# A decode step on one core: page sums taken in quarters ahead of the weight splits, the sample's output and branch A's heads moved

## The reference

```
proj = einsum('bsd,de->bse', rmsnorm(x), w_in)
q, k, v, g_a, u, v_s, g_b, m_a, m_b = split(proj)
attn   = moba(q, k, v, ...)            # branch A, 8 heads of 64
sgu    = gelu(u) * (tril(w_s) @ layernorm(gelu(v_s)) + b_s)   # branch B
y_a, y_b = attn * silu(g_a), sgu * silu(g_b)
mixed  = sigmoid(m_a) * (y_a @ w_pa) + sigmoid(m_b) * (y_b @ w_pb)
out    = rmsnorm(x + mixed @ w_o)
```

## Time and profile before

| | |
|---|---|
| median of 3 runs | 613.47 us |
| the profiled execution's own time | 611.43 us |
| its span, first to last instruction | 609.5 us |
| mean granted clock of PE | 0.992 |
| PE busy | 575.8 us, 94% of the span, 6242 matmuls |
| DVE busy | 313.1 us, 51%, 690 instructions |
| ACT busy | 215.4 us, 35%, 470 instructions |
| DMA, hardware queue | 55.9% of 16 engines' span |

### The profile page before, as it was taken

How to read it: one execution, slowest core, us unless ns; L and a number is a source line. 1 busy time by engine, 2 the same in 40 slices (tenths; PEclk the granted TensorE clock), 3 DMA queues, 4 the chain that set the end, 5 groups by cost and what they waited for, 6 DMA issues and landing times.

```text
span 609.5 us, 15236 instructions
## 1 busy us (share of the span) xinstructions
PE 575.8 (94%) x6242; PEld 540.3 (89%) x6242; DVE 313.1 (51%) x690; ACT 215.4 (35%) x470; POOL 28.9 (5%) x40
## 2 busy tenths in 40 slices
PE   3799998999999999999999999999999989999993
PEld 2799998999899989989889988998999979999993
DVE  5533131434555744855766574694463263692316
ACT  5422321233434423454354541241153241233243
POOL 1310121100000000000000000011000000000002
PEclk9999998999999999999999999999999999999998
DMA  8437333455766767568576668884779857222103
GB/s 289 129 86 279 106 108 105 126 160 186 221 182 207 225 200 243 181 195 254 174 223 203 188 222 248 274 252 157 239 261 317 257 158 260 88 95 94 46 0 147
DMA packets 73990, 112.50 MB, mean 185 GB/s; under 512 B 5417, under 2 KB 38194, under 8 KB 73922
## 3 DMA queue, kind: packets, MB, share of 16 engines
q1 hardware_dynamic: 72690, 108.18, 55.9%
q0 software_dynamic: 1232, 3.36, 1.8%
HBM read 106.98 MB, written 4.53 MB: 183 GB/s over the span
## 4 chain that ended last, share of the span: by engine, by line
PE 80%; DVE 12%; ACT 4%; issue 2%; DMA 1%; POOL 0%; DVEq 0%; SPq 0%; ACTq 0%; POOLq 0%
PE BK L470 47%; PE BK L590 8%; PE BK L490 7%; PE BK L602 4%; PE BK L616 4%; PE BK L666 2%; DVE WL L1022 1%; PE BK L683 1%; PE BK L673 1%; DMA XR<-in_x_prompt 1%; DVE XR L1043 1%; ACT SC L913 1%; DVE NMX L1210 1%; ACT APX L926 1%; PE BK L642 1%
## 5 line engine op out<-in xcount | busy, mean ns | idle before, releaser
L470 PE MATMUL BK<-XH,WH 128*128 128x272 f32 x704 | 224.3, 319 | 1.6 <-POOL WL L1455 1.6
L470 PE MATMUL BK<-XH,WL 128*128 128x272 f32 x704 | 204.5, 291 | 0.0
L470 PE MATMUL BK<-XL,WH 128*128 128x272 f32 x704 | 203.5, 289 | 0.0
L470 PEld LDWEIGHTS BK<-XH,WH 128*128 128x128 f32 x704 | 133.9, 190 | 12.4 <-issue 9.2
L470 PEld LDWEIGHTS BK<-XL,WH 128*128 128x128 f32 x704 | 134.4, 191 | 0.5 <-issue 0.5
L470 PEld LDWEIGHTS BK<-XH,WL 128*128 128x128 f32 x704 | 133.7, 190 | 0.0
L1022 DVE TENSOR_TENSOR WL<-WRAW,WH 128x1024 fp32r<-128x1024 f32 x58 | 71.0, 1224 | 96.5 <-ACT WH L815 96.3
L590 PE MATMUL BK<-CST,KRAW 128*128 128x128 f32 x512 | 77.1, 273 | 2.4 <-DVE ATS L1196 2.2
L1116 DVE COPY KT<-BK 128x512 f32<-128x512 f32 x64 | 44.2, 691 | 57.0 <-PE BK L590 56.9
L815 ACT ACTIVATE WH<-WRAW 128x1024 fp32r<-128x1024 f32 x60 | 63.2, 1054 | 21.3 <-PE BK L490 21.3
L590 PEld LDWEIGHTS BK<-CST,KRAW 128*128 128x128 f32 x512 | 60.1, 140 | 4.4 <-issue 4.1
(11 more groups left out here) (186 smaller groups left out, 780.3 us busy)
## 6 DMA issues: line engine op xcount, KB each, us to landing
KRAW<-in_cache_k SPq DMA_DIRECT2D x128, 256.0 KB, 3.3
VRAW<-in_cache_v SPq DMA_DIRECT2D x120, 256.0 KB, 3.8
WRAW<-in_w_in SPq DMA_DIRECT2D x22, 1024.0 KB, 5.5
WRAW<-in_w_o SPq DMA_DIRECT2D x4, 1024.0 KB, 5.2
XR<-in_x_prompt SPq DMA_DIRECT2D x4, 512.0 KB, 6.7
VEX<-in_cache_v SPq DMA_DIRECT2D x8, 256.0 KB, 4.0
WRAW<-in_w_pb SPq DMA_DIRECT2D x4, 512.0 KB, 6.8
WRAW<-in_w_pa SPq DMA_DIRECT2D x4, 512.0 KB, 5.9
```

The source lines that it names most:

```text
L470: last = mm(BK[h][:, 0:HALF], w[:, n % 2, k, :], x[:, k, cols], start=(i == 0 and w is WH and x is XA), stop=(i == KC - 1 and w is WL))
```

## The change

DVE's `block_sums` becomes `page_sums`, which after each fourth step's scores reduces those four pages (128 elements a row) to a sum and a maximum; after the fourth quarter it adds the bias of the last page and goes on to `gate_rows`, as before. It stands, with `prompt_out`, in front of `split_lo`. `sample_out` moves from t % 16 = 6 to 5 (the last one, t = 140, stays), ahead of that step's gelu and spatial work. On ACT, `exponentials` goes ahead of `gelu_tanh`. The heads of branch A are split in four pieces at t = 133 to 136 instead of one at t = 130, and PE's waits count the pieces.

```diff
--- before.py
+++ after.py
@@ -736,7 +736,7 @@
                 for u in range(16):
                     n, x, h = unit_of(u)
                     if u < 2:
-                        pe.wait_ge(yal_ok, u + 1)
+                        pe.wait_ge(yal_ok, PAIRS + u)
                     yield from branch(n, x, h, 16 + u, XH, XL)
 
             fill = filling()
@@ -957,10 +957,10 @@
                     page_out(t)
                 if t % 4 == 1 and 53 <= t < 85:
                     gelu_square((t - 53) // 4)
+                if t % 16 == 2 and t > 16 and t < 144:
+                    exponentials(t // 16 - 1)
                 if t % 4 == 2 and 54 <= t < 86:
                     gelu_tanh((t - 54) // 4)
-                if t % 16 == 2 and t > 16 and t < 144:
-                    exponentials(t // 16 - 1)
                 if t % 4 == 3 and 19 <= t < 83:
                     prompt_exp(t // 4 - 4)
                 if t % 4 == 0 and 20 <= t < 84:
@@ -968,10 +968,12 @@
                 if t == 111:
                     act.wait_ge(yb_ok, 5)
                     copy(YBH[:], G[:, GB:GB + 4, :]).then_inc(ybh_ok, 1)
-                if t == 130:
+                if 133 <= t < 133 + PAIRS:
+
+                    c = t - 133
                     act.wait_ge(av_ev, 16)
                     act.wait_ge(pj, matmuls_before(T_PB))
-                    copy(XH[:, 0:4, 0:SEQ], G[:, GA:GA + 4, 0:SEQ]).then_inc(yah_ok, 1)
+                    copy(XH[:, c, 0:SEQ], G[:, GA + c, 0:SEQ]).then_inc(yah_ok, 1)
                 if t == 141:
                     act.wait_ge(ya_ok, 1)
                     copy(XH[:, 0:4, SEQ:ROWS], G[:, GA:GA + 4, SEQ:ROWS]).then_inc(yah_ok, 1)
@@ -1142,13 +1144,24 @@
                 dve.wait_ge(ge_dve, 2 * (4 + c) + 2)
                 dve.tensor_tensor(G[:, GB + c], G[:, GB + c], G[:, GU + c], ALU.mult).then_inc(ug_ok, 1)
 
-            def block_sums(b):
-                dve.wait_ge(sc_pe, 4 * b + 4)
-                sc = SCB[:].rearrange("p (x n) -> p x n", x=4)
-                link(dve.tensor_reduce(KP[:, 0, :], sc, AX.X, ALU.add))
-                last_page = SCB[96:128, 3 * P:4 * P]
-                link(dve.tensor_tensor(last_page, last_page, B15, ALU.add))
-                link(dve.tensor_reduce(KP[:, 1, :], sc, AX.X, ALU.max))
+            def page_sums(q):
+
+                b, x = q // 4, q % 4
+                dve.wait_ge(sc_pe, q + 1)
+                if x == 0:
+                    wait(dve, r_ok, b)
+                sc = SCB[:, x * P:(x + 1) * P]
+                summed = dve.tensor_reduce(KP[:, 0, x:x + 1], sc, AX.X, ALU.add)
+                if x == 3:
+                    link(summed)
+                    last_page = SCB[96:128, 3 * P:4 * P]
+                    link(dve.tensor_tensor(last_page, last_page, B15, ALU.add))
+                peak = dve.tensor_reduce(KP[:, 1, x:x + 1], sc, AX.X, ALU.max)
+                if x == 3:
+                    link(peak)
+                    gate_rows(b)
+
+            def gate_rows(b):
                 own, pair, kp = CST[:, C_OWN:C_OWN + 4], CST[:, C_PAIR:C_PAIR + 2], KP[:]
                 dve.tensor_tensor(R[:, 0:8].rearrange("p (x j) -> p x j", x=4), bass.AP(pair.tensor, pair.offset, [list(pair.ap[0]), [0, 4], [1, 2]]),
                                   bass.AP(kp.tensor, kp.offset, [list(kp.ap[0]), [1, 4], [0, 2]]), ALU.mult)
@@ -1318,6 +1331,11 @@
                 if t % 4 == 0 and 4 <= t <= 128:
                     if T_GA <= n - 1 < T_GMA or T_GB <= n - 1 < T_GMB:
                         silu(n - 1, 1)
+                if t % 4 == 0 and 4 <= t <= PAGES:
+                    page_sums(t // 4 - 1)
+                if t % 4 == 0 and 20 <= t < 84:
+                    prompt_out(t // 4 - 5)
+                if t % 4 == 0 and 4 <= t <= 128:
                     split_lo(n + 1)
                 if t % 4 == 2 and t < 128 and (T_GA <= n < T_GMA or T_GB <= n < T_GMB):
                     silu(n, 0)
@@ -1330,7 +1348,7 @@
                     dve.wait_ge(ot_ev, NB)
                     dve.tensor_tensor(G[:, GA:GA + 4, SEQ:ROWS], G[:, GA:GA + 4, SEQ:ROWS], ATS[:], ALU.mult).then_inc(ya_ok, 1)
                 if t == 142:
-                    dve.wait_ge(yah_ok, 2)
+                    dve.wait_ge(yah_ok, PAIRS + 1)
                     dve.tensor_tensor(XL[:, 0:4, SEQ:ROWS], G[:, GA:GA + 4, SEQ:ROWS], f32(XH[:, 0:4, SEQ:ROWS]), ALU.subtract).then_inc(yal_ok, 1)
                 if t % 16 == 2 and t >= 34:
                     scale_out(t // 16 - 2)
@@ -1340,18 +1358,14 @@
                     page_out(t)
                 if t % 4 == 2 and 22 <= t < 86:
                     prompt_gate(t // 4 - 5)
-                if t % 16 == 6 and t >= 38:
-                    sample_out(t // 16 - 2)
-                if t % 16 == 0 and t >= 16 and t < 144:
-                    block_sums(t // 16 - 1)
                 if t % 16 == 1 and t >= 16 and t < 144:
                     choose(t // 16 - 1)
+                if t % 16 == 5 and t >= 37:
+                    sample_out(t // 16 - 2)
                 if t % 4 == 2 and 18 <= t < 82:
                     prompt_max(t // 4 - 4)
                 if t % 4 == 3 and 19 <= t < 83:
                     prompt_norm(t // 4 - 4)
-                if t % 4 == 0 and 20 <= t < 84:
-                    prompt_out(t // 4 - 5)
                 if t % 4 == 1 and 53 <= t < 85:
                     gelu_inner((t - 53) // 4)
                 if t % 4 == 3 and 55 <= t < 87:
@@ -1371,9 +1385,10 @@
                 if t == 111:
                     dve.wait_ge(ybh_ok, 1)
                     dve.tensor_tensor(YBL[:], G[:, GB:GB + 4, :], f32(YBH[:]), ALU.subtract).then_inc(ybl_ok, 1)
-                if t == 130:
-                    dve.wait_ge(yah_ok, 1)
-                    dve.tensor_tensor(XL[:, 0:4, 0:SEQ], G[:, GA:GA + 4, 0:SEQ], f32(XH[:, 0:4, 0:SEQ]), ALU.subtract).then_inc(yal_ok, 1)
+                if 133 <= t < 133 + PAIRS:
+                    c = t - 133
+                    dve.wait_ge(yah_ok, c + 1)
+                    dve.tensor_tensor(XL[:, c, 0:SEQ], G[:, GA + c, 0:SEQ], f32(XH[:, c, 0:SEQ]), ALU.subtract).then_inc(yal_ok, 1)
                 if t >= 129:
                     mixed_b(t - 129)
             mixed_b(15)
```

## The result

The changed kernel takes 614.28 us (median of 20 runs, 611.93 to 617.38), the kernel before 611.32 (20 runs, 610.0 to 614.92). The ratio on record for the two is **1.0033, 95% interval 1.0018 to 1.0049**: slower by 2.0 us of 611, with 1.1 to 3.0 as the interval. The two medians are 3.0 us apart, at the interval's upper end; I go by the ratio. Its profiled execution took 613.03 us, its span is 611.1 us against 609.5, PE is busy 575.2 us of it (575.8 before).

A forecast was written before the change was run, and what follows sets the result against it. PE is busy 94% of the span, so only its waits move the time. Lost 4.9 us, won 4.7, net +0.2 on the 613.47 median: 613.7 us, range 611.8 to 616.4.

The forecast's parts named there:

- prompt gate, t = 66: PE's 0.9 us wait for the prompt gate stays but shrinks by 0.18 us, counted as -0.2.
- gate sums, t = 17 to 20: PE comes to the choice 0.55 us earlier at t = 17 but waits 0.5 there: 0.05 us won.
- exponentials, t = 81 to 83: ACT's exponentials ahead of gelu's tanh cut PE's lateness from 1.10 to 0.04 us: -1.2 us.
- after page 127: PE's wait for page sums at t = 129 goes, 0.43 us; branch A's heads in pieces win 0.3 us.
- The new wait behind the prompt copy: At t = 20, 36, 52, 68 the split delays LT, making PE's page turning 1.13 us late each: +4.5 us.
- The later choice: DVE's gate copy GS comes 0.2 us later, delaying PE's prompt gate at t = 34 and 50: +0.4 us.
- The quarters' price: Each DVE reduction of 128 elements was taken to cost 0.286 us; quarters by themselves cost nothing where DVE is idle.
- rival (b): DVE falls behind in more places if a quarter's reduction costs 0.68 us, deciding from about 0.32: 616.0 us; chance 0.17.
- the sample's output one step earlier: PE's two waits for ATS go, 1.48 us at t = 85 and another 1.05 late: -2.5 us.
- Rival (a): Earlier sums reach the exponentials, so the waits at t = 99, 115, 131 go, 2.8 us: 610.9 us; chance 0.15.
- Rival (c): The clock falls after each of the four new waits, 1.7 us each, +6.7: 620.4 us; chance 0.08.
- Rival (d): Sums in front free nobody; gains and losses both stay under 1 us: 613.5 us; chance 0.05.

The follow-up runs named there:

- (2): Kernel before with only DVE's prompt copy put ahead of the weight split at t % 16 = 4 (four steps): ratio 1.0057.
- (1): Kernel before with only the quarter sums, placed in front of the weight split: ratio 0.9981.
- (8): Kernel before with only ACT's exponentials ahead of gelu's tanh: ratio 0.9978.
- experiment 4: Kernel before with only the sample's output taken out one step earlier: ratio 0.9978.
- 5: Changed kernel with SP's loads of mixing weights, gating constants and layernorm rows at t = 83 instead of 84: ratio 1.0009 against the kernel before.
- 7: Kernel before with the sample's output one step earlier and SP's loads of mixing weights and constants at t = 83: ratio 0.9944.
- experiment 9: Kernel before with only branch A's heads split in four pieces at t = 133 to 136: ratio 0.9994.
- experiment 10: Kernel of 6 with, at t = 97, 113, 129, gate sums ahead of page turning and choice ahead of page copy: ratio 0.9909 against the kernel before.
- 3: Changed kernel with the weight split back ahead of the prompt copy at t % 16 = 4: ratio 0.9952 against the kernel before.
- 6: Changed kernel with the split back ahead of the prompt copy at t % 16 = 4 and the loads at t = 83: ratio 0.9930 against the kernel before.

## Why the prediction was right, and where not

The prediction was 613.7 us and no change that can be told, with a range that holds the 614.28 measured. It gave most to "same" (0.53), and more to slower (0.29) than to faster (0.18). The lean was right, but its number was too kind: +0.2 us worked out, +1.47 in the trace from the first page, and a ratio whose interval, 0.18% to 0.49%, lies almost wholly past the 0.2% I had set as the limit of "same".

```
step                          worked out   trace     single experiment
pages 21, 37, 53, 69 (LT)       +4.5       +4.57     +4.5 (2)
prompt gate, t = 34, 50         +0.4       +0.44
prompt gate, t = 66             -0.2       -0.23
gate sums, t = 17 to 20          0.0        0.0      0.0 (1)
exponentials, t = 81 to 83      -1.2       -1.38     -1.14 (8)
output, t = 86, 102             -2.5       -2.58     -2.53 (4)
mixing weights, t = 87            -        +1.42     gone with the load moved (5, 7)
after page 127                  -0.7       -0.71     -0.20 of it the pieces (9)
```

The trace's column is the page table above, cut at the steps; the numbers in brackets are the experiments.

- **The new wait behind the prompt copy** was right in place, number and size. LT's end and the release 0.15 us behind it came as worked out.
- **The later choice** was right too. GS follows the prompt turning by APT, WL and KT, each overlapped by 0.09, as the changed kernel's DVE rows show beside the earlier trace rows:

```profile
201.59 0.69 DVE L1238 COPY APT<-BK 128x512 f32<-128x512 f32 x1 [0.83 <-PE BK L673]
202.20 1.22 DVE L1024 TENSOR_TENSOR WL<-WRAW,WH 128x1024 fp32r<-128x1024 f32 x1
203.33 0.68 DVE L1118 COPY KT<-BK 128x512 f32<-128x512 f32 x1
203.93 0.17 DVE L1173 COPY GS<-BK 128x24 f32<-128x24 f32 x1
```

- **The quarters' price**: 0.286 was taken for a reduction; the changed kernel has

```profile
L1154 DVE TENSOR_REDUCE KP<-BK 128x1 f32<-128x128 f32 x32 | 9.3, 291 | 46.3 <-PE BK L602 46.3
...
L1159 DVE TENSOR_REDUCE KP<-BK 128x1 f32<-128x128 f32 x32 | 9.1, 283 | 0.3
```

so rival (b), which needed over 0.32, falls, and the thin margins at t = 84 and 116 held.
- **The step that failed** is "the sample's output one step earlier: the 1.48 us go ... -2.5 us in all". The waits went, but what is late next was not looked for. It was a load on SP's queue, issued at t = 84 behind four value pages, that in the trace of before had landed 0.2 us ahead of its reader at t = 87. With 1.42 us for it the sum would have been +1.6 us, 615.1 against the median I started from.
- **At t = 17 to 20** the sum was right, one part of it was not named: of the gain at the gate sums, 0.55 worked out and 0.57 in the trace, some 0.25 us is lost at once at page 18, which waits for GS, and the other 0.3 at t = 19.
- Rival (a) falls: the waits at t = 99, 115 and 131 stayed, 0.37, 0.81 and 1.70 us late as before, until experiment 10 moved the gate sums themselves.
- Rival (c) falls: the granted clock is 1.00 after each of the four new waits (in the stretches 164 to 168, 216 to 220, 268 to 272 and 320 to 324 us). Rival (d) falls with the sizes above.

That the level of the runs moved, from 613.47 in three runs to 611.32 in twenty, has nothing to do with the change; the last section shows two causes of such differences, though not which of them made those three runs high. By the new level the forecast of +0.2 would read 611.5 and the +1.47 of the trace 612.8. So it is partly luck that 613.7 lies so near the measured 614.28: the level carried over was 2 us too high, and the sum 1.3 us too low by the trace. The trace accounts for 1.5 of the 2.0 us that the ratio gives; the other 0.5 lies within its interval, and no run here settles whether there is more in it.

## What to carry to other kernels

A wait that is taken away is only won if everything that PE reaches sooner is ready sooner, and a table of waits doesn't list what was ready with 0.2 us to spare: before counting the gain, look for the next reader of each load behind that place, and compare its landing, in more than one execution: here it moved by 1.1 us. On an engine that works in order, put what waits for another engine behind what can run now, unless somebody is waiting for it; here a 1.2 us weight split that nobody needed for another 7 us, put behind a waiting copy, made the matmul engine wait four times. Measure such small edits from a mark behind the noisy start, not by the whole span.

## What the runs showed of the hardware

The first 113 us differ between executions of the same instructions by up to 3.2 us, in two separate places, and both are the clock. After the wait of 1.7 us at L568 the granted clock (third number from the end) fell in the changed kernel's execution:

```profile
100.00:104.00 4.00, 3.46 (x20) 3.46 (x21) 0.45 (x2) 0.00 (x0) 1.29 (x2) 0.73 0.78 276
104.00:108.00 4.00, 4.00 (x29) 4.00 (x29) 1.03 (x1) 1.34 (x2) 0.00 (x0) 0.85 0.02 4
```

while in experiment 4, after the same wait of 1.74 us, it did not:

```profile
100.00:104.00 4.00, 2.26 (x19) 1.98 (x18) 1.61 (x4) 0.40 (x1) 1.29 (x2) 1.00 0.74 243
104.00:108.00 4.00, 4.00 (x34) 4.00 (x34) 0.59 (x1) 1.34 (x2) 0.00 (x0) 1.00 0.26 92
```

It fell to the lower of its two levels, 1.2 GHz, for 3.4 us (at half the clock, 0.73 and 0.85 over 4 us each make 2.2 and 1.2) in 7 of the 13 profiled executions, before and after among them, and the earlier trace rows prices it at 1.7 us. The other place is the start: the trace's first record of the full 2.4 GHz is at 23.1 to 25.0 us in nine executions and at 28.4 to 29.6 in the other four (experiments 3, 4, 6 and 7), and there the hundredth matmul starts at 32.9 to 33.5 us, where it starts at 31.1 to 31.5 in the nine. The two chances make up most of the spread before the first page. In the loop of pages nothing of the kind is left but the landing of SGC: before and experiment 9, which differ in nothing up to t = 129 and both had SGC in time, stay within 0.11 us of each other over the 128 pages.

The four new waits of 1.0 us each had matmuls close before and behind them, and the clock stayed at its upper level after each. The Trainium skill (TensorE: Matmul & The Clock Gate, HAM oscillation) has small idle times between groups of matmuls make the clock swing. For the one wait of 1.7 us the runs agree in about every other execution; for the waits of 1.0 us none does.
